# Moving means of a pooling mixer: window additions on VectorE against a second product with a banded time matrix

## The reference

```python
def _pool_mixer(h, w_grp, scale):
    hf = h.astype(F32).reshape(Bn, T, POOL_GROUPS, POOL_GROUP)
    for gi, w in enumerate(POOL_WINDOWS):
        xg = hf[:, :, gi]
        cs = jnp.cumsum(jnp.pad(xg, ((0, 0), (w, 0), (0, 0))), axis=1)
        win_sum = cs[:, w:] - cs[:, :T]
        cnt = jnp.minimum(t + 1, w).astype(F32)[None, :, None]
        outs.append(win_sum / cnt - xg)
    pooled = jnp.stack(outs, axis=2).astype(h.dtype)
    y = jnp.einsum('btgc,gcd->btgd', pooled, w_grp)
    return y.reshape(Bn, T, D) * scale
```

## Time and profile before

| | us |
|---|---|
| three runs | 2871.28, 2874.73, 2874.77 |
| median | 2874.73 |
| span of the profiled execution | 2873.1 |
| TensorE busy in it | 2625.0 (91%) |
| VectorE busy | 1768.9 (62%) |
| ScalarE busy | 1084.6 (38%) |
| GpSimd busy | 36.7 (1%) |

### The profile page before, as it was taken

One profiled execution on the slowest core, in us unless ns is written; L12 is line 12 of the kernel. 1 busy time (PEld: TensorE's weight loads), 2 busy tenths in 40 slices (PEclk: granted clock), 3 DMA queues, 4 the chain that ended last, 5 costly groups with the idle time before them and its releaser, 6 DMA issues.

```text
span 2873.1 us, 32419 instructions
## 1 busy us (share of the span) xinstructions
PE 2625.0 (91%) x13232; PEld 2192.6 (76%) x13232; DVE 1768.9 (62%) x2428; ACT 1084.6 (38%) x1475; POOL 36.7 (1%) x48
## 2 busy tenths in 40 slices
PE   5987889999479999899888999999999887999998
PEld 4776768888358888688587888888888665788887
DVE  6785688787788877711495555335534576464464
...
GB/s 318 215 77 1 103 176 278 226 183 167 19 100 189 194 208 200 82 103 59 10 1 23 44 68 66 71 55 66 69 64 53 37 23 15 66 96 110 88 104 80
DMA packets 80276, 295.07 MB, mean 103 GB/s; under 512 B 8944, under 2 KB 11632, under 8 KB 79872
## 3 DMA queue, kind: packets, MB, share of 16 engines
...
...
## 4 chain that ended last, share of the span: by engine, by line
PE 82%; DVE 11%; ACT 4%; issue 2%; POOL 1%; DMA 0%; DVEq 0%; ACTq 0%; SPq 0%
PE ps L314 68%; PE ps L340 3%; PE ps L768 2%; PE ps L2515 1%; PE ps L1924 1%; PE ps L2483 1%; DVE gatt L795 1%; DVE w_lo L292 1%; DVE h_lo L522 1%; DVE p_lo L2785 1%; DVE anm L2767 1%; DVE x L1472 1%; PE ps L1117 1%; DVE x L1485 0%; PE ps L1911 0%
## 5 line engine op out<-in xcount | busy, mean ns | idle before, releaser
L314 PE MATMUL ps<-h_hi,w_hi 128*128 128x512 f32 (+1 forms) x2416 | 816.6, 373 | 65.7 <-DVE w_lo L292 40.3
L314 PE MATMUL ps<-h_hi,w_lo 128*128 128x512 f32 (+1 forms) x2416 | 806.2, 369 | 0.0
L314 PE MATMUL ps<-h_lo,w_hi 128*128 128x512 f32 (+1 forms) x2416 | 806.0, 369 | 0.0
L292 DVE TENSOR_TENSOR w_lo<-w_raw,w_hi 128x1024 fp32r<-128x1024 f32 (+2 forms) x323 | 414.7, 1284 | 557.1 <-ACT w_hi L284 556.0
L284 ACT ACTIVATE w_hi<-w_raw 128x1024 fp32r<-128x1024 f32 (+2 forms) x323 | 357.4, 1107 | 870.4 <-PE ps L314 837.4
L314 PEld LDWEIGHTS ps<-h_hi,w_hi 128*128 128x128 f32 x2416 | 457.6, 189 | 152.8 <-DVE w_lo L292 45.9
L314 PEld LDWEIGHTS ps<-h_lo,w_hi 128*128 128x128 f32 x2416 | 458.1, 190 | 77.4 <-issue 3.1
L314 PEld LDWEIGHTS ps<-h_hi,w_lo 128*128 128x128 f32 x2416 | 457.5, 189 | 77.0
L314 PE MATMUL ps<-g_hi,w_hi 128*128 128x512 f32 (+1 forms) x880 | 295.9, 369 | 0.8 <-DVE w_lo L292 0.8
L314 PE MATMUL ps<-g_lo,w_hi 128*128 128x512 f32 (+1 forms) x880 | 295.1, 368 | 0.0
L314 PE MATMUL ps<-g_hi,w_lo 128*128 128x512 f32 (+1 forms) x880 | 295.0, 368 | 0.0
...
## 6 DMA issues: line engine op xcount, KB each, us to landing
w_raw<-in_up SPq DMA_DIRECT2D x176, 512.0 KB, 3.6
m_raw<-in_w_mod SPq DMA_DIRECT2D x96, 512.0 KB, 3.6
...
m_raw<-in_ada_w SPq DMA_DIRECT2D x83, 512.0 KB, 4.5
w_raw<-in_in SPq DMA_DIRECT2D x39, 512.0 KB, 3.7
w_raw<-in_out SPq DMA_DIRECT2D x16, 512.0 KB, 3.5
m_start<-in_ada_w SPq DMA_DIRECT2D x13, 512.0 KB, 11.7
w_raw<-in_qkv SPq DMA_DIRECT2D x12, 512.0 KB, 3.6
```

The lines of the kernel that those rows point to most:

```text
L292: dve.tensor_tensor(k.w_lo[s][:, 0:w], k.w_raw[s][:, 0:w], k.w_hi[s][:, 0:w].bitcast(F32), ALU.subtract).then_inc(*k.tick("w_lo", g))
L314: last = pe.matmul(ps[:, bank, 0:tn], a[:, c, :], b[:, c, t0:t0 + tn], start=c == 0 and n == 0, stop=c == kt - 1 and n == 2)
```

## The change

The order of the two linear steps is turned round. The group product comes first, with h as the stationary operand, so that its result has tokens on partitions (`pe_pool_values`, 24 products of 256 columns for each group). ScalarE and VectorE split that result into high and low parts out of PSUM (`act_mixed_high`, `dve_mixed_low`). The moving mean minus one is then a second product over tokens with a constant banded matrix (`pe_pool_time`): for each tile and each block of 128 tokens two products of 128 columns with the block's own strip and two of 16 columns with the strip that reaches over from the block before (in the first block one of 16 with the low part of the strip). The strips are loaded where the corrections were, 128 x 1088 values. The residual's x is scaled by GpSimd for all eight tiles, no longer by ScalarE. The running sums of x and of squares on VectorE go; TensorE adds them up as eight products with ones for each sum (`pe_pool_sums`), two tiles ahead of the last two time products and six behind them. The pool weights are four tiles of 512 columns in place of eight of 256.

```diff
-    run("pool", "pool", 0, KD, 2)
+    run("pool", "pool", 0, GROUPS, 4)
...
-        self.ph, self.recip = pm("pool_h", [P, KD, LAT]), pm("pool_recip", [P, 4, WINDOW])
+        self.pool_raw = pm("pool_raw", [P, GROUPS, STRIP])
+        self.pool_hi, self.pool_lo = pm("pool_hi", [P, GROUPS, STRIP], F32R), pm("pool_lo", [P, GROUPS, WINDOW], F32R)
         self.pgate = pm("pool_gate", [P, KD])
-        self.wins = [pm(f"pool_win{i}", [P, LAT])[:, :] for i in range(8)]
+        self.mixed_hi, self.mixed_lo = ([pm(f"mixed_{n}{i}", [P, LAT // P, 2 * P], F32R) for i in range(2)] for n in ("hi", "lo"))
...
-        dve.wait_ge(*k.seen("x_scaled", (which - 1, KD - 1)))
+        dve.wait_ge(*(k.seen("pool_scaled", KD - 1) if which == 2 else k.seen("x_scaled", (0, KD - 1))))
...
-    sp.dma_start(k.recip[:, :, :], k.ins["recip"]).then_inc(*k.tick("load", "recip", 16))
+    sp.dma_start(k.pool_raw[:, :, :], k.ins["pools"]).then_inc(*k.tick("load", "pools", 16))
...
+def pool_added(f):
+    return "taken", BASE["pool"] + f // 2 if f % 2 else ("pool", f)
+def pool_scaled(k):
     pool = k.nc.gpsimd
+    for f in range(KD):
+        x = k.x[:, f, LATS]
         pool.wait_ge(*k.seen("modulated", (("ln", 1), f)))
+        pool.tensor_scalar(x, x, k.coef[:, 2, 1, f:f + 1], k.coef[:, 3, 1, f:f + 1], ALU.mult, ALU.add).then_inc(*k.tick("pool_scaled", f))
...
+def pe_pool_values(k, g):
+    pe, tile = k.nc.tensor, BASE["pool"] + g
+    pe.wait_ge(*k.seen("w_lo", tile))
+    if g >= 2:
+        pe.wait_ge(*k.seen("h_lo", ("pool", g - 2, 1)))
+    for c in range(2):
+        pe.wait_ge(*k.seen("h_lo", (("ln", 1), 2 * g + c)))
+    for i in range(LAT // P):
+        at = slice(CTX + i * P, CTX + (i + 1) * P)
+        for c in range(2):
+            wh, wl = (w[tile % 2][:, c * 2 * P:(c + 1) * 2 * P] for w in (k.w_hi, k.w_lo))
+            hh, hl = (h[:, 2 * g + c, at] for h in (k.h_hi, k.h_lo))
+            for n, (a, b) in enumerate(((hh, wh), (hh, wl), (hl, wh))):
+                last = pe.matmul(values_of(k, g, i), a, b, start=c == 0 and n == 0, stop=c == 1 and n == 2)
+        if i == 1:
+            last.then_inc(*k.tick("product", ("pool", g)))
+    last.then_inc(*k.tick("product", tile))
+def pe_pool_time(k, f):
+    pe, g = k.nc.tensor, f // 2
+    vh, vl = (v[g % 2][:, :, (f % 2) * P:(f % 2 + 1) * P] for v in (k.mixed_hi, k.mixed_lo))
+    out, NT = k.ps[:, pooled_bank(f), :], LAT // P
+    pe.wait_ge(*k.seen("h_lo", "pools"))
+    pe.wait_ge(*k.seen("h_lo", ("pool", g, 1)))
+    if f >= 2:
+        pe.wait_ge(*k.seen(*pool_added(f - 2)))
+    own, next_one = (lambda i: k.pool_hi[:, g, P if i else 0:2 * P if i else P]), k.pool_hi[:, g, 2 * P:]
+    for i in range(NT):
+        pe.matmul(out[:, i * P:(i + 1) * P], vh[:, i, :], own(i), start=i == 0, stop=False)
+        last = pe.matmul(out[:, i * P:(i + 1) * P], vl[:, i, :], own(i), start=False, stop=False)
+        if i == 0:
+            pe.matmul(out[:, 0:WINDOW], vh[:, i, :], k.pool_lo[:, g, :], start=False, stop=False)
+        else:
+            for v in (vh, vl):
+                last = pe.matmul(out[:, i * P:i * P + WINDOW], v[:, i - 1, :], next_one, start=False, stop=i == NT - 1 and v is vl)
+    last.then_inc(*k.tick("turn", ("pooled", f)))
+def pe_pool_sums(k, f):
+    pe, st = k.nc.tensor, ("ln", 2)
+    pe.wait_ge(*k.seen("centered", (st, f)))
+    total = pe.matmul(k.ps[:, 5, 0:LAT], k.ones[:, :], k.x[:, f, LATS], start=f == 0, stop=f == KD - 1)
+    if f == KD - 1:
+        total.then_inc(*k.tick("summed", (st, "mean")))
+    pe.wait_ge(*k.seen("squared", (st, f)))
+    pe.matmul(k.ps[:, 7, 0:LAT], k.ones[:, :], k.tmp[f % 2][:, :], start=f == 0, stop=f == KD - 1
+              ).then_inc(*(k.tick("summed", (st, 1)) if f == KD - 1 else k.tick("summed", (st, "pool", f))))
 def pe_pool(k):
+    st = ("ln", 2)
+    pe_pool_values(k, 0)
+    pe_pool_values(k, 1)
+    for f in range(2):
+        pe_pool_time(k, f)
+    pe_pool_values(k, 2)
+    k.nc.tensor.wait_ge(*k.seen(*pool_added(0)))
+    k.nc.tensor.matmul(k.ps[:, 5, 0:LAT], k.ones[:, :], k.x[:, 0, LATS], start=True, stop=True).then_inc(*k.tick("guessed", st))
+    for f in range(2, 4):
+        pe_pool_time(k, f)
+    pe_pool_values(k, 3)
+    for f in range(4, 6):
+        pe_pool_time(k, f)
+    for f in range(2):
+        pe_pool_sums(k, f)
+    for f in range(6, 8):
+        pe_pool_time(k, f)
+    for f in range(2, KD):
+        pe_pool_sums(k, f)
+    pe_filler(k, 14)
+def act_mixed_high(k, g):
+    act = k.nc.scalar
+    for half in range(2):
+        act.wait_ge(*(k.seen("product", BASE["pool"] + g) if half else k.seen("product", ("pool", g))))
+        if g >= 2:
+            act.wait_ge(*k.seen("turn", ("pooled", 2 * g - 3)))
+        act.activation(k.mixed_hi[g % 2][:, 2 * half:2 * half + 2, :].rearrange("p i d -> p (i d)"), k.ps[:, 2 * (g % 2) + half, :], ACT.Copy
+                       ).then_inc(*k.tick("h_hi", ("pool", g, half)))
+def act_pool_square(k, f):
+    act, st = k.nc.scalar, ("ln", 2)
+    act.wait_ge(*k.seen("centered", (st, f)))
+    if f >= 2:
+        act.wait_ge(*k.seen("summed", (st, "pool", f - 2)))
+    act.activation(k.tmp[f % 2][:, :], k.x[:, f, LATS], ACT.Square).then_inc(*k.tick("squared", (st, f)))
+def act_pool(k):
+    act, base, st = k.nc.scalar, BASE["pool"], ("ln", 1)
+    act.wait_ge(*k.seen("summed", (st, "mean")))
+    act.activation(k.rstd[:, LATS], k.ps[:, 5, 0:LAT], ACT.Square, scale=1.0 / D).then_inc(*k.tick("mean_squared", 1))
+    act_split(k, base + 1)
+    act.wait_ge(*k.seen("variance", 1))
+    act.activation(k.rstd[:, LATS], k.rstd[:, LATS], ACT.Ln, bias=k.col("eps5")).then_inc(*k.tick("root_log", st))
+    act.wait_ge(*k.seen("root_log", st))
+    act.activation(k.rstd[:, LATS], k.rstd[:, LATS], ACT.Exp, scale=-0.5).then_inc(*k.tick("root", st))
+    act.wait_ge(*k.seen("load", "pools"))
+    act.activation(k.pool_hi[:, :, :], k.pool_raw[:, :, :], ACT.Copy).then_inc(*k.tick("h_hi", "pools"))
+    act.wait_ge(*k.seen("coef", (1, 1)))
+    for f in range(KD):
+        act.wait_ge(*k.seen("scaled", (1, f)))
+        act_modulated(k, 1, f)
+        if f in (4, 6):
+            act_mixed_high(k, f // 2 - 2)
+            act_split(k, base + f // 2)
+    act_mixed_high(k, 2)
+    act_split(k, base + 4)
+    act_guess(k, ("ln", 2))
+    for f in range(2):
+        act_pool_square(k, f)
+    act_mixed_high(k, 3)
+    for f in range(2, KD):
+        act_pool_square(k, f)
+    act_split(k, base + 5)
+def dve_mixed_low(k, g):
     dve = k.nc.vector
+    for half in range(2):
+        dve.wait_ge(*k.seen("h_hi", ("pool", g, half)))
+        at = k.mixed_hi[g % 2][:, 2 * half:2 * half + 2, :].rearrange("p i d -> p (i d)")
+        if g >= 2:
+            dve.wait_ge(*k.seen("turn", ("pooled", 2 * g - 3)))
+        dve.tensor_tensor(k.mixed_lo[g % 2][:, 2 * half:2 * half + 2, :].rearrange("p i d -> p (i d)"), k.ps[:, 2 * (g % 2) + half, :],
+                          at.bitcast(F32), ALU.subtract).then_inc(*k.tick("h_lo", ("pool", g, half)))
+def dve_pool_add(k, f):
+    dve, x = k.nc.vector, k.x[:, f, LATS]
+    dve.wait_ge(*k.seen("turn", ("pooled", f)))
+    dve.wait_ge(*k.seen("pool_scaled", f))
+    dve.scalar_tensor_tensor(x, k.ps[:, pooled_bank(f), :], k.pgate[:, f:f + 1], x, ALU.mult, ALU.add).then_inc(*k.tick(*pool_added(f)))
+def dve_pool_center(k, f):
+    dve, st, x = k.nc.vector, ("ln", 2), k.x[:, f, LATS]
     if f == 0:
+        dve.wait_ge(*k.seen("guess", st))
+    dve.wait_ge(*k.seen(*pool_added(f)))
+    dve.tensor_tensor(x, x, k.mean[:, :], ALU.subtract).then_inc(*k.tick("centered", (st, f)))
...
+    dve, base, st = k.nc.vector, BASE["pool"], ("ln", 1)
+    dve_split(k, base + 1)
+    dve.wait_ge(*k.seen("summed", (st, 1)))
+    dve.wait_ge(*k.seen("mean_squared", 1))
+    dve.scalar_tensor_tensor(k.rstd[:, LATS], k.ps[:, 7, 0:LAT], 1.0 / D, k.rstd[:, LATS], ALU.mult, ALU.subtract
+                             ).then_inc(*k.tick("variance", 1))
+    dve.tensor_scalar(k.mean[:, :], k.ps[:, 5, 0:LAT], 1.0 / D, None, ALU.mult).then_inc(*k.tick("mean", 1))
+    dve.tensor_tensor(k.pgate[:, :], k.mods1[:, 1, 2 * KD:3 * KD], k.col("pool_scale", 0, KD), ALU.mult).then_inc(*k.tick("pool_gate"))
+    dve.wait_ge(*k.seen("mean", 1))
+    for f in range(2):
+        dve_recenter(k, 1, f)
+    dve.wait_ge(*k.seen("root", st))
+    for f in range(KD + 1):
+        if f < KD:
+            x = k.x[:, f, LATS]
+            dve.wait_ge(*k.seen("recentered", (1, f)))
+            dve.tensor_tensor(x, x, k.rstd[:, LATS], ALU.mult).then_inc(*k.tick("scaled", (1, f)))
+        if f == 0:
+            dve.wait_ge(*k.seen("h_hi", "pools"))
+            dve.tensor_tensor(k.pool_lo[:, :, :], k.pool_raw[:, :, 0:WINDOW], k.pool_hi[:, :, 0:WINDOW].bitcast(F32), ALU.subtract
+                              ).then_inc(*k.tick("h_lo", "pools"))
+            dve.wait_ge(*k.seen("pool_gate"))
+        if f + 2 < KD:
+            dve_recenter(k, 1, f + 2)
+        if f:
```

(36 more changed lines are left out.)

88 lines of the change are left out of this document (18 added, 70 removed).

## The result

The changed kernel took 2854.13 us (median of 9; the kernel before beside it 2873.83, also 9): a ratio of 0.994, 95% interval 0.9924 to 0.9956. That is some 17 us less by the ratio, and 19.7 by the two medians. Two further series gave 0.9936 (0.9912 to 0.996) and 0.9937 (0.9918 to 0.9957). Executions of one kernel differ by up to 19 us (before 2868.7 to 2886.3, changed 2849.5 to 2868.3), so the medians of the changed kernel vary between series (2854.1, 2857.8, 2857.5).

The account below looks back on a forecast made before the run. VectorE bounds, then TensorE: from 753.4 its list of 11.5 + 0.9 + 21.6 + 14.1 = 48.1 us, plus 1.8, 0.6 and 0.2, ends at 804.1 against 812.74, 8.6 less: 2866.1 us, range 2857 to 2873.

Parts of the forecast that it names:

- What goes, and the bound: Between the two variances: 24.3 us of VectorE instructions go, some 32 us of path in all; the bound moves to TensorE.
- The price of the time products: TensorE's eight time products: 0.235 us per 128-column instruction, 0.117 per 16-column one, 21.6 us in all.
- Rival (a): Time products: all 15 instructions a tile cost 0.117 us each; stage ends at 798.2, 14.5 less, 2860.2; chance 0.29.
- Its cheaper end: Time products at 0.06 us an instruction: 17.4 us less, 2857.3.
- GpSimd beside VectorE: Norm tiles ahead of the first product: each GpSimd scaling delays VectorE 0.85 us (0.5 to 1.05), two on the path.
- its sign of a later start: GpSimd's scaling well over 1.05 us would delay VectorE's norm tiles and TensorE's start by two such lengths.
- Rival (d): Ahead of first product: GpSimd does not hold VectorE; TensorE starts 1.7 earlier, 10.8 us less, 2863.9; chance 0.48 shared with forecast.
- The clock: Start of TensorE's list: lower clock for some 3.5 us, half of it lost, 1.8 us.
- Rival (c): Group and time products all at 1.2 GHz: stage ends 32 us later, 2898; chance 0.12 including anything else slower.
- The head: Before variance 1: splitting the second pool tile there adds 1.0 us on the path; first normed tile follows 2.53 later.
- The sums as products: Norm sums: 14 running sums, 9.7 us, leave VectorE; 16 TensorE products at 0.88 us, 14.1 us, come.
- What follows is unchanged: Behind the stage, norm tiles and up-projection: no change; TensorE idles and falls to the lower clock as before.

## Why the prediction was wrong, step by step

- **What goes, and the bound** (right). VectorE lost 23.9 us and TensorE became the late engine, gapless from 752.4. The sums went 0.86 apart (0.88 said), their tail took 10.4 (10.6 said), VectorE stood idle for 8.08 in it (some 8).
- **The price of the time products** (the step that failed). It took 0.235 for 128 columns, the price of the plain fillers, and 0.117 for 16: 2.70 us a tile, 21.6 in all. Measured: 1.63 and 13.0, so 8.6 too much. One product with its weight load took 0.108 us, whether all were 128 columns wide or seven of fifteen 16. Variance 2 came at 796.17, or 795.9 less the 0.27 by which the stage began later, 8.2 sooner than the 804.1 forecast; the other terms that were off, below, cancel but for 0.4. The earlier trace rows had the answer twice. A plain product stands there as two instructions, and the filler row counts 28 instructions for 14 products, so 0.117 was the price of one instruction of that width, and a rounded product is one instruction. And the rounded products of 256 columns come out at 0.12 there, as they measured in the changed kernel: the prediction gave half their width nearly twice their price. It named 0.117 as its lower bound and took the higher one because the fillers were "of the same shape". That 0.117 came so near is in part luck: at 512 columns one plain instruction took 0.44 and a rounded one 0.23. The estimate from the Trainium skill (TensorE: Matmul & The Clock Gate, Back-to-back issue gap), 9.7 us for the 120 instructions, was too low by 3.3 but nearer than the sum; the measurement is 0.108 an instruction.
- **Rival (a)** is what happened: 0.117 each, 798.2 said, 795.9 measured. It counted 1.7 us of waits for VectorE; TensorE had none (no gap from 752.39 on). Its cheaper end, 17.4 us less at 0.06, does not follow from the terms shown: 14.4 us fewer of time products make 23.0, and the 5.6 between, presumably waits for VectorE, are not worked out, though the low end of the range hangs on it.
- **GpSimd beside VectorE** (right in kind, too large). A multiply took 1.10 instead of 0.68, 0.42 of delay where 0.85 was taken (bounds 0.5 to 1.05, so outside them). Two such delays were put ahead of the first product, and only one fell there (749.94); the difference, 1.3 us, is all of what TensorE started early (752.39, or 752.1 less the 0.27, instead of 753.4). GpSimd's operation took 0.77 alone (769.00) and 2.24 (median) beside VectorE's norm instructions: it was GpSimd that waited most, and the subtraction and the low part beside it kept their 0.68. The subtraction that reads PSUM (757.52) and the GpSimd operation beside it kept 0.69 and 0.77, so it cost the path nothing. The Trainium skill (SBUF — State Buffer, Who interferes with whom) says that of two such instructions the one issued first blocks the other. The rows fit that: both engines' instructions were stretched. So the price for VectorE was not the length of GpSimd's operation, as the prediction had it: the scaling came well over 1.05, its sign of a later start, and TensorE started sooner than said. Undone, it was worth nothing at the end of the stage. Rival (d), without this delay, is given 10.8 us less, where its own 1.7 on top of 8.6 make 10.3.
- **The clock.** 1.8 us of surcharge at the start was forecast. The lower level lasted 5.5 us there, not 3.5, but cost 0.4, as VectorE's low parts held TensorE as long anyway. What was not foreseen is the second fall, 1.0 to 1.5 us. Rival (c), the clock staying down through the group and time products, did not come; it was seen only where TensorE was made to wait (0.52 over 17.5 us with all sums on VectorE).
- **The head** (right). Variance 1 is 0.90 later behind the last add (1.0 said), the first multiply 2.53 behind it (2.53 said).
- **The sums as products** (wrong in what it credits). It subtracted 9.7 us of running sums from VectorE's path. Alone they bring 0.3 us (69.65 to 69.31), and on top of the other two parts 0.8 to 1.4 once TensorE is kept busy in its wait (52.75 against 51.4 to 51.9), 1.2 of which are late fillers.
- **What follows is unchanged** (right for the stage's neighbours). Of the 3.5 us beyond the stage in the profiled pair, 2.8 are a clock difference at one place. Two profiles of the changed kernel differ by more, 8 us in one stretch, without any edit; that these differences are chance was not tested.
